# Start bytes of four split operand tiles of a two-block network on one NeuronCore

## The reference

```
first block (272 tokens)
  layer 0: h += gla_mixer(rmsnorm(h))          # gated linear attention; (o * silu(r)) @ w_out
           h += (silu(gate) * up) @ ffn_w_out  # D_FF = 2816; gate, up = rmsnorm(h) @ ffn_w_in
  layer 1: h += dsa_mixer(rmsnorm(h))          # attention 1, 8 heads, top-64 keys
           h += (silu(gate) * up) @ ffn_w_out
  h = rmsnorm(h) without the 16 tokens
second block (256 tokens)
  layer 0: h += (gelu(gate) * rg_lru(conv(rec))) @ a_w_out
           h += square(relu(h @ w_up)) @ w_down            # inner width 4096
  layer 1: h += chunk_band_attention(q, k, v) @ b_w_o      # attention 2, 16 heads
           h += square(relu(h @ w_up)) @ w_down
```

## Time and profile before

| what | value |
|---|---|
| time, median of 2 runs | 1182.38 us (1182.01 to 1182.76) |
| profiled execution, first to last instruction | 1182.2 us |
| TensorE busy | 1169.6 us, 99% |
| VectorE / ScalarE busy | 819.2 us / 691.5 us |
| weights and inputs loaded | 205.66 MB, 175 GB/s over the span |
| mean granted TensorE clock | 0.998 |

### The profile page before, as it was taken

The page is one execution under the profiler, slowest core; times in us unless marked ns, Lnnn a source line. Parts: engine busy times, 40 slices in busy tenths (PEclk is TensorE's granted clock), DMA queues, the critical chain, the costliest instruction groups (busy, mean ns, idle before and its releaser), DMA issues. The chain is left out here.

```text
span 1182.2 us, 25988 instructions
## 1 busy us (share of the span) xinstructions
PE 1169.6 (99%) x9738; PEld 1140.9 (97%) x9738; DVE 819.2 (69%) x1296; ACT 691.5 (58%) x1115; POOL 89.5 (8%) x97
## 2 busy tenths in 40 slices
PE   8999999999999999999999999999999999999998
PEld 8999999999998899999999989999999979999998
DVE  7767866665577877666668997675567677776543
ACT  6635765654455567666556976664447576666432
POOL 1000200000110020000120000000013223000000
PEclk9999999999999999999999999999999999999999
DMA  7532655555664336555664556666666424566663
GB/s 270 177 94 89 193 178 177 177 178 192 200 202 144 107 107 190 191 190 193 209 209 155 193 180 192 191 193 191 206 212 205 142 77 153 185 193 193 202 195 106
DMA packets 57577, 207.84 MB, mean 176 GB/s; under 512 B 6352, under 2 KB 7568, under 8 KB 57248
## 3 DMA queue, kind: packets, MB, share of 16 engines
q1 hardware_dynamic: 57136, 203.52, 54.6%
q0 software_dynamic: 288, 3.21, 0.7%
q10 hardware_dynamic: 80, 0.07, 0.0%
HBM read 205.66 MB, written 1.05 MB: 175 GB/s over the span
## 5 line engine op out<-in xcount | busy, mean ns | idle before, releaser
L1679 DVE TENSOR_TENSOR w_lo<-w_raw,w_hi 128x1024 fp32r<-128x1024 f32 x379 | 463.4, 1225 | 68.7 <-ACT w_hi L511 68.1
L511 ACT CAST w_hi<-w_raw 128x1024 fp32r<-128x1024 f32 x379 | 395.1, 1045 | 174.1 <-PE acc L1006 172.2
L1004 PE MATMUL acc<-x_hi,w_hi 128*128 128x256 f32 (+1 forms) x1688 | 479.0, 284 | 2.2 <-DVE w_lo L1679 1.5
L1005 PE MATMUL acc<-x_lo,w_hi 128*128 128x256 f32 (+1 forms) x1688 | 473.3, 280 | 0.0
L1006 PE MATMUL acc<-x_hi,w_lo 128*128 128x256 f32 (+1 forms) x1688 | 473.2, 280 | 0.0
L1004 PEld LDWEIGHTS acc<-x_hi,w_hi 128*128 128x128 f32 x1688 | 317.8, 188 | 6.0 <-DVE x_lo L1699 1.8
L1005 PEld LDWEIGHTS acc<-x_lo,w_hi 128*128 128x128 f32 x1688 | 317.7, 188 | 0.5
L1006 PEld LDWEIGHTS acc<-x_hi,w_lo 128*128 128x128 f32 x1688 | 317.6, 188 | 0.0
L1004 PE MATMUL acc<-m_hi,w_hi 128*128 128x256 f32 x512 | 141.3, 276 | 0.0
L1005 PE MATMUL acc<-m_lo,w_hi 128*128 128x256 f32 x512 | 141.3, 276 | 0.0
L1006 PE MATMUL acc<-m_hi,w_lo 128*128 128x256 f32 x512 | 141.3, 276 | 0.0
(11 more groups left out here) (370 smaller groups left out, 1671.3 us busy)
## 6 DMA issues: line engine op xcount, KB each, us to landing
w_raw<-weights SPq DMA_DIRECT2D x381, 512.0 KB, 4.0
bias<-bias_rows POOLq DMA_DIRECT2D x1, 2048.0 KB, 8.7
h<-hT SPq DMA_DIRECT2D x4, 272.0 KB, 4.5
bias<-bias_rows POOLq DMA_DIRECT2D x1, 1088.0 KB, 8.9
outT<-h SPq DMA_DIRECT2D x4, 256.0 KB, 4.6
con<-constants SPq DMA_DIRECT2D x1, 913.0 KB, 9.3
w_raw<-weights SPq DMA_DIRECT2D x2, 256.0 KB, 3.1
par<-cols SPq DMA_DIRECT2D x1, 84.0 KB, 2.0
```

The costliest lines, as they stand in the source:

```text
L511: nc.scalar.copy(w_hi[:, slot, :], w_raw[:, slot, :]).then_inc(hi_ready, 1)
L1004: nc.tensor.matmul(out, wh, xh[:, k, tok], start=first and n == 0, stop=False)
L1005: nc.tensor.matmul(out, wh, xl[:, k, tok], start=False, stop=False)
L1679: V.tensor_tensor(w_lo[:, slot, :], w_raw[:, slot, :], w_hi[:, slot, :].bitcast(F32), ALU.subtract)\
```

## The change

`mid_pad` and `m_pad` (192 bytes each) go ahead of `mid_hi` and `m_hi`, so that both pairs begin at 0 (bytes 128,512 and 123,904) and all their rows are at 0. `at_pad` grows from 160 to 192 bytes: `at_hi` and `at_lo` are at 96. `lr_pad` grows from 160 to 288 bytes: `lr_hi` and `lr_lo` are at 192. `ga_hi` and `ga_lo` begin where they did (at 64), but their rows take 1088 bytes and no longer 1280, so the eight rows are at 64, 128, 192, 0 and again 64, 128, 192, 0; `ga_pad` fills the bytes that `ga_hi` gives up. `ga_lo` gives up as many (1536, six times 256), so the tiles behind it move by that. `sqg`, behind `mid_lo`, moves by 192 bytes. No instruction, wait, order or size changes.

```diff
--- before.py
+++ after.py
@@ -200,8 +200,9 @@
 
 
         stack, get = region()
-        ga_hi = get("ga_hi", [P, KD, ROW], F32R)
-        ga_lo = get("ga_lo", [P, KD, ROW], F32R)
+        ga_hi = get("ga_hi", [P, KD, T], F32R)
+        ga_pad = get("ga_pad", [P, KD * (ROW - T)])
+        ga_lo = get("ga_lo", [P, KD, T], F32R)
         k_T = get("k_T", [P, 4, T])
         v_T = get("v_T", [P, 8, T])
         q_T = get("q_T", [P, 4, T])
@@ -229,6 +230,7 @@
         up_s = get("up_s", [P, 2, T])
         silu_s = get("silu_s", [P, 2, T])
         mid_s = get("mid_s", [P, 2, T])
+        mid_pad = get("mid_pad", [P, 48])
         mid_hi = get("mid_hi", [P, 24, ROW], F32R)
         mid_lo = get("mid_lo", [P, 24, ROW], F32R)
         sqg = get("sqg", [P, KD, T])
@@ -260,7 +262,7 @@
         nmx1 = get("nmx1", [P, 2 * ATT_HEADS])
         rs1 = get("rs1", [P, 2 * ATT_HEADS])
         ri1 = get("ri1", [P, 2 * ATT_HEADS])
-        at_pad = get("at_pad", [P, 40])
+        at_pad = get("at_pad", [P, 48])
         at_hi = get("at_hi", [P, ATT_HEADS, SEQ], F32R)
         at_lo = get("at_lo", [P, ATT_HEADS, SEQ], F32R)
         stack.close()
@@ -276,7 +278,7 @@
         t_s = get("t_s", [P, KD, SEQ])
         b_s = get("b_s", [P, KD, SEQ])
         gelu_s = gate2
-        lr_pad = get("lr_pad", [P, 40])
+        lr_pad = get("lr_pad", [P, 72])
         lr_hi = get("lr_hi", [P, KD, SEQ], F32R)
         lr_lo = get("lr_lo", [P, KD, SEQ], F32R)
         stack.close()
@@ -285,6 +287,7 @@
         stack, get = region()
         y_s = get("y_s", [P, 2, SEQ])
         y2_s = get("y2_s", [P, 2, SEQ])
+        m_pad = get("m_pad", [P, 48])
         m_hi = get("m_hi", [P, FF2T, SEQ], F32R)
         m_lo = get("m_lo", [P, FF2T, SEQ], F32R)
         stack.close()
```

## The result

The changed kernel takes 1197.83 us (1197.39 to 1198.27, 2 runs) against 1182.38 us. The ratio of the runs is 1.0122, with a 95% interval from 1.0106 to 1.0138: it is 1.2% slower, where 1177.1 us and a range up to 1195 were forecast. By span the loss is 1196.3 - 1182.2 = 14.1 us. (Those 1196.3 us belong to an execution of 1198.27 us, so some 2 us lie outside a span. The 0.2 us that the prediction took for that set the span of one execution against the median of others; probably for the same reason the medians differ by 15.4 us and the spans by 14.1.)

The account below looks back on a forecast made before the run. TensorE, busy 99% of the span, was taken to bound the kernel through its matmul pitch. Terms -4.1 - 1.1 + 0.1 + 0.6 - 0.8 = -5.3 us took the span from 1182.2 to 1176.9; plus 0.2, 1177.1 us, range 1169 to 1195.

Parts of the forecast that it names:

- What bounds the kernel: Whole kernel: TensorE is busy 99% of the span, so a stage lasts as long as its matmuls one after another.
- Items 6 and 7: Writers and readers of moved tiles elsewhere: taken at nothing; weight loads, ScalarE and VectorE stay covered behind a faster TensorE.
- Item 1: `m` and layer 1's `mid`, 256 columns moved to 0: 2 ns less for each of 2,064 matmuls, -4.1 us.
- The bounds, 108.4 and 120.0: Pitch limits in ns for 256-column middles at 0: plain f32 overhead (-10.1 us) and behaviour as at 128 (+13.8 us).
- Item 2: Layer 0's `mid`, 272 columns moved to 0: 2 ns less for each of 528 matmuls, -1.1 us.
- Item 3: `ga` with rows at 64, 128, 192, 0: +0.6 ns for each of 192 matmuls, +0.1 us.
- Item 4: `at` at 96, taken half way between 64 and 128: +3.2 ns for each of 192 matmuls, +0.6 us.
- Item 5: `lr` at 192, 64 bytes from the weights on the other side: 113.3 ns in place of 117.7, -0.8 us.
- The slow mode: Rival, chance 0.24: middles at 0 start in a lasting 117.7 ns mode; +12.1 us in all, 1194.5 us.
- As bad as at 128: Rival, chance 0.04: middles at 0 cost +6.7 ns a matmul; +18.1 us with `at` and `ga`, 1200.5 us.
- The point from which slower was to follow: Threshold for the middles: the kernel gets slower once the mean pitch at 0 is over about 113.5 ns.
- The Trainium skill's rule: TensorE has two independent read ports and never waits, so start bytes cost nothing and the time stays 1182.4 us.

Follow-up runs that it names:

- without the odd row: Kernel before, with the last of the eight rows of `x` at 64 like the other seven, not 64 bytes off: 1188.55 us, ratio 1.0045.
- the run with `w_lo` alone: Kernel before, with `w_lo` at 192 instead of 128, `w_hi` unmoved, and in layer 1 `m_lo` and `mid_lo` at 128: 1212.49 us (one run).

## Why the prediction was wrong

*What bounds the kernel* held: no wait grew, and 14.4 us of pitch make 14.1 us of span. Items 6 and 7 held too.

*Item 1*, the 2,064 middles of 256 columns, is the step that failed: "I take 2 more", from 113.3 to 111.3 ns. They took 118.7, so +11.1 us in place of -4.1. The step read three points (120.0 at distance 0, 113.3 at 64, a floor of 108.4) as a fall with distance. The runs at ten starts show no such fall; 113.3 was seen only at 64 bytes to either side and only in one of two modes, and the trace of before had hinted at it, since two of its tiles at the same 64 ran at 117.7. The bounds, 108.4 and 120.0, did hold the value. The lower one was never approached by a float32r stage in any run.

*Item 2* (272 columns): taken at -2 ns, measured +3.4, +1.8 us; same mistake. *Item 3* (`ga`): the sign was right, the size not: +2.8 ns and not +0.6. *Item 4* (`at`): +4.9 ns against +3.2; the half way between two rows was too little, since 96 measured 118.4. *Item 5* (`lr`): no gain, 118.0 after against 117.7. The 113.3 that it hoped for does exist 64 bytes above the weights, but this stage, like `m` at 192, didn't run in that mode; and the 117.7 that it started from was a mode too, since `lr` at its old place showed 113.3 for a while in other traces. Summed by these steps: 11.1 + 1.8 + 0.5 + 0.9 = 14.4 us against -5.3.

*The rivals.* The slow mode, with 1194.5 us, came nearest and ended on the right side, for a reason half right, so its nearness is partly luck: two modes exist, and a stage inherits its mode (`x` and `mid` without the odd row). But the changed kernel's middles weren't in an inherited slow mode; they were entered from `x` at 114, and at distance 128 no fast mode was found. By span its sum was 2.0 us too low (12.1 against 14.1; the middles gave +12.9 and not +11.4), and the median lies 1.5 us above the profiled span where the prediction put 0.2; this is why 1197.8 fell outside a range that ended at 1195. "As bad as at 128" (1200.5) was given 0.04 though the result lies between the two. The point from which slower was to follow, 113.5 ns, was right.

*The Trainium skill's rule* ("SBUF — State Buffer", "Who interferes with whom") is that TensorE never waits on anyone. It holds here as far as other engines go: with all of them idle the pitch stayed at 118.7. What that section also says, that TensorE's two read ports are independent, is hard to fit with this: with the moving rows left in place and the weights moved by 64 bytes, `x` went from 114 to 120 ns. The other rule of the Trainium skill ("TensorE: Matmul & The Clock Gate", "Wait — 56ns, not 53.3ns?"), N / 2.4 GHz plus 2.5 ns, was reached by no float32r stage in any run; the best was 113.3.

*Open:* by what means the weights' start acts on the streaming row. That it does, and without any other engine, is shown. Which load meets which stream is not, since the run with `w_lo` alone fitted neither pairing. That two reads of TensorE get in each other's way, as the prediction put it, remains an inference. It also stays open what sets the mode at a stage's entry, and why 48 and 80 are so much worse than 64.

## What to carry to other kernels

When one engine is busy from end to end, read its pitch from first and last starts, by tile and by stage: busy shares and medians of durations hide differences of 4% that are the whole result. If equal matmuls show two pitches in one trace, the better one may be a state and not a property of the layout; don't extrapolate from it to a layout not seen, and price the change from the worse one too. A start byte is worth sweeping on the chip, always together with the start of the weights, and a candidate needs many runs, since the mode entered can differ from one to the next.

## What the runs showed of the hardware

Float32r matmuls of 256 columns at the full granted clock (1.00 in the windows) took from 113.3 to 120.0 ns apart, by start bytes alone, and 272 columns from 123.3 to 126.7. Moving weights and rows together by 64 bytes changed nothing (1.0002). At 64 bytes below the weights two modes, 113.3 and 117.8 ns, each held for a whole stage of hundreds of matmuls, through changes of tile, until a wait or an odd row; 64 bytes above them both were seen as well (113.3 for 21 matmuls, 117.8 for a whole stage). The pitch of the slow layout was the same, 118.7 ns, with VectorE, ScalarE and the DMA at work and with all of them idle. 16 bytes more or less (48 and 80) gave 119.2, among the slowest.
